# A transformer kernel of three blocks on one NeuronCore: the first modulated layer's gate sums move from TensorE to ScalarE and GpSimd

## The reference, cut to what matters

```python
silu_c = jax.nn.silu(c)
for i in range(DEPTH_2):
    mod = silu_c @ ada_w[i] + ada_b[i]            # [1, 6 * 1024]
    sh1, sc1, g1, sh2, sc2, g2 = [m[:, None, :] for m in jnp.split(mod, 6, axis=-1)]
    h = rms_norm(x, norm_mix_g[i]) * (1.0 + sc1) + sh1
    ...
    x = x + g1 * y
    h = rms_norm(x, norm_ffn_g[i]) * (1.0 + sc2) + sh2
    x = x + g2 * grouped_moe(...)
```

## Time and profile before

| what | value |
|---|---|
| time, median of 3 runs | 1163.28 us (1161.19 to 1168.87) |
| span of the profiled execution, first to last instruction | 1165.4 us |
| its TensorE clock, mean of the span | 0.989 of full |
| busy share of the span: PE, DVE, ACT, POOL | 94%, 52%, 36%, 9% |

### The profile page before, as it was taken

One profiled execution on the slowest core, in us unless ns is written; L12 is line 12 of the kernel. 1 busy time (PEld: TensorE's weight loads), 2 busy tenths in 40 slices (PEclk: granted clock), 3 DMA queues, 4 the chain that ended last, 5 costly groups with the idle time before them and its releaser, 6 DMA issues.

```text
span 1165.4 us, 17160 instructions
## 1 busy us (share of the span) xinstructions
PE 1094.7 (94%) x6756; PEld 735.1 (63%) x6756; DVE 604.6 (52%) x1164; ACT 424.0 (36%) x731; POOL 101.0 (9%) x193
## 2 busy tenths in 40 slices
PE   7999899999999989989999999888999999999986
PEld 7878567899999857767544434226878754343422
DVE  3488756767878655685323233227746522322223
ACT  6445534644544445473411111006537421110100
POOL 0211123010121110030000000002000100000000
PEclk9999999999999989999999999998999999999999
DMA  9977694997999768654899999996576679999996
GB/s 295 280 248 272 223 319 148 256 336 219 350 341 281 264 236 286 230 205 155 318 411 410 408 409 410 408 402 205 178 256 235 236 293 408 409 409 409 409 409 246
DMA packets 164719, 356.14 MB, mean 306 GB/s; under 512 B 10649, under 2 KB 79513, under 8 KB 164513
## 3 DMA queue, kind: packets, MB, share of 16 engines
q1 hardware_dynamic: 147600, 295.81, 69.8%
q0 software_dynamic: 17024, 59.26, 14.8%
q10 hardware_dynamic: 16, 0.02, 0.0%
HBM read 351.89 MB, written 7.36 MB: 308 GB/s over the span
## 4 chain that ended last, share of the span: by engine, by line
PE 72%; DMA 15%; DVE 7%; ACT 3%; issue 1%; POOL 1%; SPq 1%; POOLq 0%; DVEq 0%; ACTq 0%
PE bank L616 38%; PE bank L1214 13%; PE bank L1224 6%; DMA ering<-in_moe_w_up 3%; DMA work<-in_moe_w_up 3%; DMA ering<-in_moe_w_gate 3%; PE bank L1183 2%; PE bank L787 2%; PE bank L541 2%; DMA a_raw<-in_moe_w_up 2%; DMA a_raw<-in_moe_w_down 2%; DMA ering<-in_ada_w 1%; DVE wlo L606 1%; PE bank L921 1%; PE bank L1990 1%
## 5 line engine op out<-in xcount | busy, mean ns | idle before, releaser
L606 DVE TENSOR_TENSOR wlo<-wraw,whi 128x1024 fp32r<-128x1024 f32 x150 | 179.1, 1222 | 59.7 <-ACT whi L602 59.0
L602 ACT ACTIVATE whi<-wraw 128x1024 fp32r<-128x1024 f32 x150 | 153.8, 1053 | 55.9 <-PE bank L616 52.2
L616 PE MATMUL bank<-a_hi,whi 128*128 128x256 f32 x512 | 146.2, 286 | 0.3 <-DVE wlo L606 0.3
L616 PE MATMUL bank<-a_lo,whi 128*128 128x256 f32 x512 | 144.8, 283 | 0.0
L616 PE MATMUL bank<-a_hi,wlo 128*128 128x256 f32 x512 | 144.8, 283 | 0.0
L1214 PE MATMUL bank<-ering,work 128*64 128x512 f32 x576 | 129.6, 595 | 9.8 <-DMA ering<-in_moe_w_up 5.5
L1461 DVE TENSOR_TENSOR work<-work,bank 128x512 f32<-128x512 f32 x16 | 11.0, 688 | 202.6 <-PE bank L1214 202.6
L1350 ACT ACTIVATE o_hi<-work 128x512 fp32r<-128x512 f32 x32 | 20.2, 631 | 236.0 <-DVE work L1410 235.6
L616 PE MATMUL bank<-whi,a_hi 128*128 128x512 f32 x256 | 104.5, 408 | 0.8 <-DVE wlo L606 0.8
L616 PEld LDWEIGHTS bank<-a_hi,whi 128*128 128x128 f32 x512 | 98.1, 192 | 9.1 <-issue 7.0
L1214 PEld LDWEIGHTS bank<-ering,work 128*64 128x64 f32 x576 | 40.1, 137 | 97.2 <-issue 77.3
(11 more groups left out here) (336 smaller groups left out, 1854.9 us busy)
## 6 DMA issues: line engine op xcount, KB each, us to landing
ering<-in_moe_w_up SPq DMA_DIRECT2D x36, 1024.0 KB, 18.2
ering<-in_moe_w_down SPq DMA_DIRECT2D x36, 1024.0 KB, 18.0
ering<-in_moe_w_gate SPq DMA_DIRECT2D x36, 1024.0 KB, 17.4
work<-in_ada_w POOLq DMA_DIRECT2D x44, 512.0 KB, 7.7
ering<-in_ada_w POOLq DMA_DIRECT2D x38, 512.0 KB, 5.0
wraw<-in_w_in SPq DMA_DIRECT2D x28, 512.0 KB, 7.5
wraw<-in_a_w_qkv SPq DMA_DIRECT2D x24, 512.0 KB, 5.3
work<-in_moe_w_down SPq DMA_DIRECT2D x12, 1024.0 KB, 18.8
```

The costliest lines, as they stand in the source:

```text
L602: nc.scalar.activation(w_hi(c), wraw[:, c % RING, :], ACT.Copy).then_inc(w_hi_done, 1)
L606: nc.vector.tensor_tensor(w_lo(u[0]), wraw[:, u[0] % RING, :], w_hi(u[0]).bitcast(F32), ALU.subtract).then_inc(w_lo_done, 1)
L616: mm = nc.tensor.matmul(out_ap, l, r, start=first and n == 0, stop=last and n == len(terms) - 1)
```

## The change

The eight bundles of group 0 are no longer multiplied on TensorE one by one. In each of the steps 0 to 7 of the attention, ACT, between the copy of the projected unit and the copy of the transposed head, waits for the bundle and multiplies its two 128x1024 tiles by the column of silu(c), one number to a partition (`first_weigh`); bundle 0 goes into `he_raw` that way, bundles 1 to 7 are weighed in place. GpSimd adds the weighed bundles 1 to 7 to `he_raw`, two additions of 128x1024 for each, and after each bundle issues the load of the bundle two further on (`first_add`). After the first half of the z projection TensorE waits for all 14 additions and makes four products with a block of ones, one for each strip. Bundle 10's load, whose place is `he_raw`, now waits for these products, and everything behind it in GpSimd's queue with it. `grow_add(0)` waits for these products in place of the eight bundles. The remaining edits rename and merge semaphores (`small_halves`, `g_done`, `pool_done`) and correct counts.

```diff
+ADA_FIRST = range(0, 8)
+FIRST_ADDS = 2 * (len(ADA_FIRST) - 1)
-SIDE_BUNDLES = [1, 2, 3, 4, 5, 6, 7, 8, 8, 8]
...
@@ load_ada @@
+                elif m == 0:
+                    pool.wait_ge(first_weighed, 2)
+                elif m in ADA_FIRST:
+                    pool.wait_ge(pool_done, 2 * m)
                 else:
                     pool.wait_ge(ada_used, ada_count(m))
+            elif n == ADA_LATE:
+
+                pool.wait_ge(ada_used, 1)
...
+        def first_weigh(act, n):
+
+            if n == 0:
+                act.wait_ge(sil_c, 1)
+            act.wait_ge(ada_in[ada_ring(n)], 32 * ada_turn(n))
+            for h in range(2):
+                dst = he_raw[:, h, :] if n == 0 else ada_part(n, h)
+                nc.scalar.activation(dst, ada_part(n, h), ACT.Copy, scale=silc[:, n, 0:1]).then_inc(first_weighed, 1)
+
+        def first_add(pool, n):
+
+            for h in range(2):
+                acc = he_raw[:, h, :]
+                pool.wait_ge(first_weighed, 2 * n + h + 1)
+                if n >= 2:
+                    pool.wait_ge(pool_done, 2 * (n - 2) + h + 1)
+                nc.gpsimd.tensor_tensor(acc, acc, ada_part(n, h), ALU.add).then_inc(pool_done, 1)
...
@@ GpSimd @@
-            for n in range(2, ADA_BLOCK):
+            for n in ADA_FIRST:
+                if n >= 1:
+                    first_add(pool, n)
+                load_ada(pool, n + 2)
+            for n in range(ADA_LATE, ADA_BLOCK):
...
@@ TensorE @@
-            bundles = [0]
+            bundles = [ADA_FIRST.stop]
...
-            attention_pe(pe, 0, side_units, side_bundles)
+            attention_pe(pe, 0, side_units)
...
-            pe.wait_ge(g_done, 1)
-            pe.wait_ge(gbm_done, 1)
+            pe.wait_ge(pool_done, FIRST_ADDS)
+            for q in range(4):
+                mm = nc.tensor.matmul(psum[ADA_BANK[0]][32 * q:32 * q + 32, :], con[:, C_ONES:C_ONES + 32],
+                                      he_raw[:, q // 2, (q % 2) * HALF:(q % 2 + 1) * HALF], start=True, stop=True)
+            mm.then_inc(ada_used, 1)
+            pe.wait_ge(g_done, 2)
...
@@ ScalarE, side_act @@
                         nc.scalar.activation(cin[:, n, 3:3 + S], psum[n % 2][:, 0:S], ACT.Copy).then_inc(g_evac, 1)
+                if i in ADA_FIRST:
+                    first_weigh(act, i)
...
@@ VectorE, grow_add @@
-                dve.wait_ge(ada_used, (8, ADA_SUM)[l])
+                dve.wait_ge(ada_used, (1, ADA_SUM)[l])
```

More of the change, by code:

```diff
@@ L463, in build_program @@
         ada_used, grow_done, acol_done = sem("ada_used"), sem("grow_done"), sem("acol_done")
+        first_weighed = sem("first_weighed")
         modc_ps, modc_bias, modc_done = sem("modc_ps"), sem("modc_bias"), sem("modc_done")
@@ L508, in ada_count @@
         def ada_count(n):
-            return n + 1 if n < ADA_BLOCK else n + 1 - len(ADA_ADDED) + (n >= ADA_NORM)
+            done = n + 2 - len(ADA_FIRST)
+            return done if n < ADA_BLOCK else done - len(ADA_ADDED) + (n >= ADA_NORM)
         ADA_SUM = ada_count(ADA_NORM) - 1
@@ L565, in rows_added @@
         def rows_added(l):
-            return 3 * SUB_POOL + 2 * (l + 1)
+            return FIRST_ADDS + 3 * SUB_POOL + 2 * (l + 1)
         def add_first_rows(pool, l):
@@ L572, in add_first_rows @@
                 pool.wait_ge(x_tmp, 4 * l + n + 1)
-                nc.gpsimd.tensor_tensor(x[:, 0, cols], x[:, 0, cols], hn[:, 0, cols], ALU.add).then_inc(sub_done, 1)
+                nc.gpsimd.tensor_tensor(x[:, 0, cols], x[:, 0, cols], hn[:, 0, cols], ALU.add).then_inc(pool_done, 1)
         def by_half(at, half):
@@ L598, in split_hi @@
             elif U_FFN + 4 <= c < U_FFN + 6:
-                act.wait_ge(ada_used, ADA_BLOCK)
+                act.wait_ge(ada_used, ada_count(ADA_BLOCK - 1))
             elif c >= U_FFN + 6:
@@ L717, in norm_sums @@
                 if n in (4, 6) and t == 0:
-                    act.wait_ge(sub_done, rows_added(n // 2 - 2))
+                    act.wait_ge(pool_done, rows_added(n // 2 - 2))
                 elif xs:
@@ L1632, in ffn_loads @@
                     load_unit(sp, (up + 1, i, m), wd[rows, :])
-            sp.wait_ge(ada_used, ADA_BLOCK - 2)
+            sp.wait_ge(ada_used, ada_count(ADA_BLOCK - 3))
             ffn_loads(0, None)
@@ L1816, in _ @@
                 v = hn[:, :, n * P:(n + 1) * P]
[L1817 to L1820, removed]
+                nc.gpsimd.tensor_tensor(sub_sq, v, v, ALU.mult).then_inc(pool_done, 1)
+                pool.wait_ge(pool_done, FIRST_ADDS + 3 * n + 1)
+                nc.gpsimd.tensor_tensor(sub_half, sub_sq[:, :, 0:64], sub_sq[:, :, 64:P], ALU.add).then_inc(pool_done, 1)
+                pool.wait_ge(pool_done, FIRST_ADDS + 3 * n + 2)
                 nc.gpsimd.tensor_tensor(sub_part[:, n, :, :], sub_half[:, :, 0:32], sub_half[:, :, 32:64], ALU.add
-                                        ).then_inc(sub_done, 1)
+                                        ).then_inc(pool_done, 1)
             add_first_rows(pool, 0)
@@ L1871, in _ @@
                                      start=True, stop=True).then_inc(small_ps, 1)
-            pe.wait_ge(small_lo, 1)
+            pe.wait_ge(small_halves, 2)
             pe.wait_ge(small_copied, 1)
@@ L2190, in _ @@
                 busy(psum[0], BUSY_WO)
-                pe.wait_ge(sub_done, rows_added(l))
+                pe.wait_ge(pool_done, rows_added(l))
                 turn_pe(pe, 5 + 3 * l, x_done, X_AT["wo", l], x, pair_cols, X_AT["wo", l] - 2)
@@ L2245, in small_split @@
                 act.wait_ge(const_in, 16 * CONST_DMAS)
-                nc.scalar.activation(sw_r[:, :, 0:16], sw[:, 0, :, :], ACT.Copy).then_inc(small_hi, 1)
+                nc.scalar.activation(sw_r[:, :, 0:16], sw[:, 0, :, :], ACT.Copy).then_inc(small_halves, 1)
             t5s = work[0:A_H, 12324:12324 + 512]
@@ L2526, in _ @@
             dve.wait_ge(const_in, 16 * CONST_DMAS)
-            dve.wait_ge(small_hi, 1)
+            dve.wait_ge(small_halves, 1)
             nc.vector.tensor_tensor(sw_r[:, :, 16:32], sw[:, 0, :, :], sw_r[:, :, 0:16].bitcast(F32),
-                                    ALU.subtract).then_inc(small_lo, 1)
+                                    ALU.subtract).then_inc(small_halves, 1)
             for l in range(2):
@@ L2607, in _ @@
             dve.wait_ge(g_done, 1)
-            nc.vector.tensor_copy(gbm, bc(M_G, 8, P)).then_inc(gbm_done, 1)
+            nc.vector.tensor_copy(gbm, bc(M_G, 8, P)).then_inc(g_done, 1)
             grow_add(0)
@@ L2796, in add_gated @@
                     if n == 3:
-                        dve.wait_ge(sub_done, rows_added(count))
+                        dve.wait_ge(pool_done, rows_added(count))
                     nc.vector.tensor_tensor(x[:, t, cols], x[:, t, cols], hn[:, t, cols], ALU.add).then_inc(x_done, 2)
@@ L2891, in sub_sums @@
                         heads = slice(0, 4) if i == A_H else slice(4, SUB_POOL)
-                        dve.wait_ge(sub_done, 3 * heads.stop)
+                        dve.wait_ge(pool_done, FIRST_ADDS + 3 * heads.stop)
                         dst = sm[:, M_OS:M_OS + 16].rearrange("p (t n) -> p n t", t=T)[:, heads, :]
```

9 lines of the change are left out of this document (3 added, 6 removed).

## The result

The changed kernel takes 1200.5 us (median of 6 runs, 1196.2 to 1201.7), the kernel before 1162.2 (6 runs, 1159.3 to 1168.9): the ratio on record is 1.030, 95% interval 1.0274 to 1.0324 (the two medians by themselves would give 1.033). It is 3% slower, 3.5 us above the forecast of 1197. The profiled execution's span is 1198.1 us against 1165.4, +32.7.

A forecast was written before the change was run, and what follows sets the result against it. The prediction took the loop DVE, ACT, DVE as the bound, 6.45 us a step, with TensorE just under it. Terms -0.2 + 1.7 + 31.5 + 1.4 = +34.4 on a span of 1165.4: 1199.8, median 1197 us (1187 to 1207).

The forecast's parts named there:

- The bundles leave TensorE: Attention of block 1: eight bundles fewer on TensorE gain 0 to 0.4 us, taken as 0.2.
- ACT weighs: ACT's sixteen Copies in the attention: 1.7 us (0 to 2.0) lost in step 0, nothing in normal steps.
- GpSimd adds: Attention steps: each addition holds DVE's instructions with both operands in SBUF, 4.5 us a bundle, 31.5 for seven.
- The product with ones: Behind the attention: four products ahead of lines 1928 and 1933 and a later copy of z, 1.4 us (1.0 to 2.0).
- rival (d): On top of the forecast TensorE's clock falls; last two units and what follows lose 6 to 13 us, 1203 to 1210; chance 0.09.
- Rival (a): In the attention DVE and GpSimd take turns but pack better: +17, 1180 us; chance 0.12.
- (b): In the attention long additions cost DVE next to nothing: +2.9, 1166 us; chance 0.12.
- (c): TensorE's share was the attention's bound after all: -8.0 + 1.0, 1156 us, faster by 0.6%; chance 0.03.

The follow-up runs named there:

- Experiment one: The changed kernel with each of GpSimd's 14 additions cut to 8 of its 1024 columns; 1168.8 us, ratio 1.0032 to the kernel before.
- seven: The kernel before with DVE's convolutions put ahead of the weight's lower half in each step; 1164.5 us, ratio 1.0003.
- eight: The changed kernel with additions cut to 8 of 1024 columns and DVE's convolutions put ahead of the lower half; 1163.7 us, ratio 0.9984.
- experiment nine: The changed kernel with 22 products that nothing reads, put only in TensorE's idle gaps at the stage's end; 1196.5 us, ratio 1.0286.
- experiment two: The changed kernel with each of GpSimd's 14 additions cut to 512 of its 1024 columns; 1185.5 us, ratio 1.0175.
- ten: The kernel before with DVE's convolutions ahead of the lower half, the same kernel as seven, in a single run; 1160.4 us.
- experiment five: The changed kernel with two more waits on GpSimd, which place each bundle's additions elsewhere in DVE's step; 1191.1 us, ratio 1.0224.
- experiment six: The changed kernel with DVE's convolutions put ahead of the weight's lower half in each step; 1189.2 us, ratio 1.0218.

## Why the prediction was right

The forecast of 1197 us lies 3.5 under the median, but that is no missing term. The sum was made for the span, 1199.8 us, and the span is 1198.1. The prediction then took 2.1 us off, the distance from the span of before to the median of its three runs; in the changed kernel the profiled execution took 1199.9 us, 1.8 above its own span, and the median lies 0.6 above that. By its own steps, in the profiled executions:

- **The bundles leave TensorE** (0.2 forecast): right, 0.4. Head 7's transposes start 0.06 us behind DVE's reciprocal, 0.43 before. Experiment one, with the bundles gone and nothing else in the way, has the period at 6.45 us; seven and eight show the condition under which more would come. Two readings were off. The step with TensorE busy 6.12 of 6.5 us was the only one with a gap, so TensorE was nearer to being the bound than I took it to be. And seven bundles where DVE sets the pace and two at the end make nine; it is six and two.
- **ACT weighs** (1.7 in step 0, elsewhere nothing): right. DVE's wait for ACT there is 2.75 us in place of 1.01. A Copy took 1.09 us, not 1.0, hidden all the same.
- **GpSimd adds** (31.5): right in kind and place (DVE held in line 2577 alone, in every one of seven steps), too large by 3.5 us. An addition took 2.48 us in place of 2.34, but held DVE for only 2.0, since DVE's own instruction of 0.485 us runs between and under them. I had taken 0.1 off for that and should have taken one instruction. This is the one term whose size was wrong by much, and the mechanism it stands for was right.
- **The product with ones** (1.4): right, 1.6. From the end of the z products to DVE's first reading of line 1964's it is 3.74 us in place of 2.11: 1.04 us in the chain, and the copy of z comes too late for line 1964's second half. No wait for GpSimd: its last pair ends at 135.1, the product starts at 157.3.
- **The clock**, which I had only as rival (d) with 0.09, was there: 4.0 us in the chain, 3.9 by experiment nine. I had argued that at 1.2 GHz TensorE's step still fits into 11 us, which held, and that only the last units and what follows count, which is where it showed. I gave it too small a chance because I took it as an extra and not as the likely consequence of an engine that stands idle 25 of 89 us, though the earlier trace rows showed the clock at 0.83 in a stretch with about the same share of idle time (2.65 of 10 us); of its 6 to 13 us the low end was half again too high. And 1.6 of the 4.0 us need not come in every execution: behind the same gap of 2.42 us the statistics' products took 5.29 us here and 5.37 in seven, but 3.67 in experiments two and ten.

Where DVE first reads line 1964's products (161.12 us against 126.67) the changed kernel is 34.45 us late, 35.06 from the stage's start, which came 0.61 us sooner. The terms give 1.7 + 28.0 + 4.0 + 1.6 - 0.4 = 34.9, and the 0.2 us that the transposes take longer when TensorE comes to them from standing still make it 35.1. The end of the span has +32.7. Of the difference, 2.2 us arise at 420 to 460 us, where in the profiled execution of before two groups (1.94 and 5.14 us in the chain) ran at the lower clock and in the one of after (1.06 and 3.77) didn't. That is chance of the two executions and belongs to neither kernel: the second of these groups took 3.77 us in seven and ten, which are the kernel before with one exchange, and 5.87 in experiment one, which is the changed kernel with short additions.

So the total came out better than its terms, and that is luck: a hold 3.5 us too large and a clock of 4.0 us left out cancel. Rival (a) is refuted for this kernel, though experiment five shows that its mechanism is real; (b) by the result itself and experiment two, (c) by experiment one. Rival (d)'s mechanism is there, with 4.0 us in place of 6 to 13.

## What to carry to other kernels

Before work goes to GpSimd, list the instructions that DVE runs beside it. Those with two SBUF inputs, and SBUF-to-SBUF TENSOR_SCALARs however small, will be held for up to the addition's length, and in experiment six some for two additions. Those that read PSUM and reductions kept their time here, and so did two-input instructions beside a GpSimd instruction that only writes; for TENSOR_SCALARs beside such a one the runs don't settle it. And an engine that is busy 96% of a stage isn't its bound unless something waits for it: here taking 8 us from it brought 0.4, and 3 to 5 us in the attention only after the engine in front of it had been freed, of which the whole run's time shows 1 to 2, not clear of noise.

## What the runs showed of the hardware that I had not expected

- One DVE instruction of 0.485 us was held for 5.40 us by two additions back to back; in other steps the two engines alternated.
- A TENSOR_SCALAR of 128x2, 0.17 us by itself, took 1.36 to 1.83 us in experiment five, until the addition beside it had ended.
- A GpSimd memset of 1024 columns, 1.016 us, cost DVE's two-input instructions nothing (0.485 us each).
- After a gap of 2.42 us the statistics' products took 5.37 us in one execution (seven) and 3.67 in another of the same kernel (ten).
